# Two transformer blocks on one core: x kept feature-major, the sums into x made with stationary weights

## What is computed

```
def rmsnorm(x, g):
    return x * rsqrt(mean(x * x, axis=-1) + 1e-6) * g

# block 0, layers l = 0, 1                      norms n = 2l, 2l + 1
h = rmsnorm(x, attn_norm[l]); x = x + concat(swa(h), pool(h), mla(h)) @ w_out[l]
h = rmsnorm(x, ffn_norm[l]);  x = x + (silu(h @ w_gate[l]) * (h @ w_up[l])) @ w_down[l]
# block 1, layers l = 0, 1                      norms n = 4 + 2l, 5 + 2l
h = rmsnorm(x, norm_mix[l]);  x = x + mixed(fox(h), nsa(h), gates(h)) @ w_out[l]
h = rmsnorm(x, norm_mlp[l]);  x = x + square(relu(h @ w_up[l])) @ w_down[l]
out = rmsnorm(x, norm_final)
```

## Time and profile before

| | us |
|---|---|
| median of 3 runs (lowest, highest) | 2890.83 (2888.51, 2895.26) |
| profiled execution | 2891.26 |
| its span, first to last instruction | 2889.1 |
| mean granted TensorE clock in it | 0.986 of full |

### The profile page before, as it was taken

The page is one execution under the profiler, slowest core; times in us unless marked ns, Lnnn a source line. Parts: engine busy times, 40 slices in busy tenths (PEclk is TensorE's granted clock), DMA queues, the critical chain, the costliest instruction groups (busy, mean ns, idle before and its releaser), DMA issues.

```text
span 2889.1 us, 34914 instructions
## 1 busy us (share of the span) xinstructions
PE 2754.8 (95%) x13625; PEld 2268.5 (79%) x13625; DVE 1501.4 (52%) x2695; ACT 1158.9 (40%) x2126; POOL 131.3 (5%) x221
## 2 busy tenths in 40 slices
PE   7999999998999999989999999999989899999997
PEld 6777888887778888867777888888767778888886
DVE  6755343357554343565766544343566665543343
ACT  4554222235542222455554343232354644342231
POOL 1000000000000000001022000000011111000000
PEclk9899999999999999999999999999999999999999
DMA  4102332321023323221311223332312211332332
GB/s 123 48 23 77 102 96 95 96 88 55 16 77 101 96 95 96 90 66 45 102 52 44 88 91 99 95 95 95 91 44 81 81 42 54 102 95 95 95 98 77
DMA packets 186358, 231.41 MB, mean 80 GB/s; under 512 B 11874, under 2 KB 140356, under 8 KB 186196
## 3 DMA queue, kind: packets, MB, share of 16 engines
q1 hardware_dynamic: 184500, 225.95, 24.8%
q0 software_dynamic: 976, 1.32, 0.3%
q10 hardware_dynamic: 720, 1.92, 0.2%
HBM read 227.05 MB, written 2.11 MB: 79 GB/s over the span
## 4 chain that ended last, share of the span: by engine, by line
PE 81%; DVE 11%; ACT 4%; issue 3%; DMA 0%; POOL 0%; DVEq 0%; ACTq 0%; SPq 0%
PE bank L643 24%; PE bank L645 23%; PE bank L644 23%; DVE Wl L2126 2%; PE bank L860 1%; PE bank L805 1%; ACT Wh L1416 1%; PE bank L881 1%; DVE STT L2405 1%; PE bank L882 1%; PE bank L742 1%; PE bank L923 1%; PE bank L924 1%; PE bank L790 1%; PE bank L1105 1%
## 5 line engine op out<-in xcount | busy, mean ns | idle before, releaser
L2126 DVE TENSOR_TENSOR Wl<-RAW,Wh 128x1024 fp32r<-128x1024 f32 (+3 forms) x434 | 511.2, 1200 | 369.9 <-ACT Wh L1416 369.0
L1416 ACT ACTIVATE Wh<-RAW 128x1024 fp32r<-128x1024 f32 (+3 forms) x434 | 438.3, 1032 | 368.0 <-PE bank L645 367.4
L643 PE MATMUL bank<-Hh,Wh 128*128 128x512 f32 (+1 forms) x976 | 393.8, 403 | 6.6 <-DVE Wl L2126 5.0
L645 PE MATMUL bank<-Hh,Wl 128*128 128x512 f32 (+1 forms) x976 | 383.5, 393 | 0.0
L644 PE MATMUL bank<-Hl,Wh 128*128 128x512 f32 (+1 forms) x976 | 383.1, 393 | 0.0
L643 PE MATMUL bank<-Wh,A 128*128 128x512 f32 x864 | 337.8, 391 | 0.0
L645 PE MATMUL bank<-Wh,A 128*128 128x512 f32 x864 | 336.8, 390 | 0.0
L644 PE MATMUL bank<-Wl,A 128*128 128x512 f32 x864 | 336.7, 390 | 0.0
L643 PE MATMUL bank<-HA,Wh 128*128 128x512 f32 x704 | 276.5, 393 | 7.5 <-DVE HA L2175 7.5
L645 PE MATMUL bank<-HA,Wl 128*128 128x512 f32 x704 | 275.4, 391 | 0.0
L644 PE MATMUL bank<-HA,Wh 128*128 128x512 f32 x704 | 275.3, 391 | 0.0
(11 more groups left out here) (370 smaller groups left out, 4272.7 us busy)
## 6 DMA issues: line engine op xcount, KB each, us to landing
RAW<-in_w_up_dram SPq DMA_DIRECT2D x108, 512.0 KB, 3.6
RAW<-in_w_down_dram SPq DMA_DIRECT2D x108, 512.0 KB, 3.8
RAW<-in_w_in_dram SPq DMA_DIRECT2D x90, 512.0 KB, 3.5
RAW<-in_w_gate_dram SPq DMA_DIRECT2D x44, 512.0 KB, 3.5
RAW<-in_w_out_dram SPq DMA_DIRECT2D x28, 512.0 KB, 3.8
RAW<-in_cmp_w_dram SPq DMA_DIRECT2D x16, 512.0 KB, 3.9
RAW<-in_w_o_fox_dram SPq DMA_DIRECT2D x8, 512.0 KB, 3.4
RAW<-in_w_o_nsa_dram SPq DMA_DIRECT2D x8, 512.0 KB, 3.4
```

The source lines that it names most:

```text
L643: pe.matmul(o, sh, mh, start=first, stop=False)
L645: return pe.matmul(o, sl, mh, start=False, stop=last)
L1416: sc.activation(M.Wh[:, v % NHL, 0:n], M.RAW[:, v % NRAW, 0:n], ACT.Copy).then_inc(G.w_hi, 1)
L2126: ve.tensor_tensor(M.Wl[:, v % NRAW, 0:n], M.RAW[:, v % NRAW, 0:n], M.Wh[:, v % NHL, 0:n].bitcast(F32), ALU.subtract).then_inc(G.w_lo, 1)
```

## The change

x becomes feature-major, `XT[128, 8, 512]`, from the first turn on.

- `lin_x` (new) makes all sums into x but those of the last feed-forward part. It has the loops of `lin_s` over the same units, but the weights are stationary and the activation moves: four banks of 128 features by 512 tokens. `add_x` adds them to XT (one DVE instruction for each bank) without a factor.
- At a last sum, ACT makes the high part of h(n) from XT right after the addition, and a square of the tile (scaled by 1/1024, no row sum) into `SQX[k]`; DVE makes the low part of the tile before. The turns of norms 1 to 7 are gone; that of n = 0 stays, with an added copy of each bank to XT on ACT.
- GpSimd adds the eight squared tiles of a norm (`add_squares`: seven additions 128x512, each waits for the one before). PE sums over the partitions by token: at the third tick of the product after the sum, four matmuls of one column with `SQS` stationary and ones moving. DVE makes the factors from that bank. The `rb` tile is made for all eight norms, four ticks later.
- The factors are now applied ahead of `down`: block 0 by one more DVE multiplication of the silu tile with rb, block 1 by taking relu on DVE with rb as second factor, with ACT squaring in its place.
- The last feed-forward part keeps `lin_s` and a token-major sum in `XO`. XT is turned back once by eight groups of four transposes (`back_side`) during its first `wide` products, and ACT copies the banks.

The core of the diff, in this order: PE's program (`pe`), ACT's (`sc`), DVE's (`ve`), GpSimd's (`gp`).

```diff
+    def lin_x(name, kt, xh, xl, before=None, often=0):
+        k0, rh, rl = 0, tiles(xh), tiles(xl)
+        while k0 < kt:
+            u, h, lo, ku = next_unit()
...
+            for j in range(NT):
...
+                for k in range(ku):
+                    if before:
+                        before(k0 + k)
+                    i = three(M.bank[bb[j][0]][:, :], h[:, k, j * P:(j + 1) * P], lo[:, k, j * P:(j + 1) * P],
+                              rh[k0 + k], rl[k0 + k], k0 + k == 0, k0 + k == kt - 1)
...
+                tick()
+            k0 += ku
     def normed(n):
         def before(k):
-            if k == 4:
-                drain(turning[n])
-            pe.wait_ge(*K.drained(f"turn{n} {k}"))
+            if n == 0 and k == 4:
+                drain(*turning)
+            pe.wait_ge(G.parted, KD * n + k + 1)
     def factor_side(n):                         
-        yield from idle(5 if n else 8)
-        if n in BY_TOKEN:
+        if n:
+            yield from idle(2)
+            b = fresh(f"ss{n}")
+            pe.wait_ge(G.sqs, 7 * n)
+            for s in range(NT):
+                i = pe.matmul(b[:, s:s + 1], M.SQS[:, s * P:(s + 1) * P], M.ONE[:, 0:1], start=s == 0, stop=s == NT - 1)
+            i.then_inc(*K.fills(f"ss{n}"))
+            yield
+            K.close(f"ss{n}")
+            yield from idle(3)
+        else:
+            yield from idle(8)
+        b = fresh(f"rb{n}")
+        pe.wait_ge(G.rstd, n + 1)
...
+    def back_side():
+        yield from idle(8)
+        for s in range(NT):
+            for half in range(2):
+                b = fresh(f"back {s}{half}")
+                for q in range(4):
+                    i = pe.transpose(b[:, q * P:(q + 1) * P], M.XT[:, 4 * half + q, s * P:(s + 1) * P], ident)
...
     def add_x(half, n=None):
-        def evac(s, name):
+        def evac(j, name):
             if n is not None:
+                k = 4 * half + j
                 sc.wait_ge(*K.drained(name))
-                square_rows(s, half)
+                sc.activation(M.h(n)[0][:, k, :], M.XT[:, k, :], ACT.Copy, scale=M.GT[:, col:col + 1]).then_inc(*hi.up())
+                sc.activation(M.SQX[k], M.XT[:, k, :], ACT.Square, scale=D ** -0.5).then_inc(G.sqx, 1)
     def turn_side(half):
...
+        for k in ks:
+            name = f"turn {k}"
+            sc.wait_ge(G.parted, k + 1)
+            sc.activation(M.XT[:, k, :], M.bank[K.of(name)][:, :], ACT.Copy).then_inc(*K.empties(name))
+    def add_x(half, n=None):
+        def part(k):
+            col = gain_column(n) + k
+            lower(M.h(n)[1][:, k, :], M.XT[:, k, :], M.h(n)[0][:, k, :], M.GT[:, col:col + 1]).then_inc(G.parted, 1)
+        def evac(j, name):
+            k = 4 * half + j
+            ve.wait_ge(*K.full(name))
+            ve.tensor_tensor(M.XT[:, k, :], M.bank[K.of(name)][:, :], M.XT[:, k, :], ALU.add).then_inc(*K.empties(name))
+            if n is not None:
+                if k:
+                    part(k - 1)
+                if k == KD - 1:
+                    part(k)
                     def product(j, name):
+                        ve.wait_ge(*silu.due())
+                        ve.tensor_tensor(m[:, j, :], m[:, j, :], M.rb(n)[:, :], ALU.mult).then_inc(*own.up())
...
+                    def relu(j, name):
...
+                        ve.scalar_tensor_tensor(m, M.bank[K.of(name)][:, :], 0.0, M.rb(n)[:, :], ALU.max, ALU.mult).then_inc(*K.empties(name))
+    def add_squares(n):
+        for k in range(1, KD):
+            gp.wait_ge(G.sqx, KD * (n - 1) + k + 1)
+            if k > 1:
+                gp.wait_ge(*added.now())
+            gp.tensor_tensor(M.SQS, M.SQX[0] if k == 1 else M.SQS, M.SQX[k], ALU.add).then_inc(*added.up())
```

More of the change, by code:

```diff
@@ L588, in norm_of @@
     return 4 * block + 2 * l + place
[L591 to L597, removed]
 def unit_of(plan, u):
@@ L1038, in ffn @@
                     lin_t(f"wide{l} {t}", KD, H[0], H[1], before)
+                if last and t == 0:
+                    back = begin(back_side())
                 before = None
@@ L1044, in down @@
             def down(half):
-                lin_s(f"down{block}{l} {c} {half}", size, A[0], A[1], 512, once(lambda k: pe.wait_ge(G.a_lo, base + k + 1)) if half == 0 else None)
+                name, split = f"down{block}{l} {c} {half}", once(lambda k: pe.wait_ge(G.a_lo, base + k + 1)) if half == 0 else None
+                if last:
+                    lin_s(name, size, A[0], A[1], 512, split)
+                else:
+                    lin_x(name, size, A[0], A[1], split)
+            if last and c == 0:
+                drain(back)
             if x0 == sum(chunks):
@@ L1503, in normed, with back_side @@
+    def factor_side(n):
+        yield from idle(7 if n else 9)
+    def back_side():
+        yield from idle(8)
+        for s in range(NT):
+            for half in range(2):
+                yield
+                name = f"back {s}{half}"
+                sc.wait_ge(*K.full(name))
+                sc.activation(M.XO[:, s, half * 512:half * 512 + 512], M.bank[K.of(name)][:, :], ACT.Copy).then_inc(*K.empties(name))
     def normed(n):
         def before(k):
-            if k == 4:
-                drain(turning[n])
+            if n == 0 and k == 4:
+                drain(*turning)
@@ L1767, in ffn, with squared @@
                 else:
[L1768 removed]
+                    def squared(j, name):
                         m = M.TMP[:, (t + j) % 7, :]
[L1770 to L1774 removed]
+                        sc.wait_ge(*K.drained(name))
+                        sc.activation(m, m, ACT.Square).then_inc(G.a_sq, 1)
+                        sc.wait_ge(*a_sq.due())
                         sc.activation(A[0][:, t + j, :], m, ACT.Copy).then_inc(*hi.up())
[L1776 to L1777 removed]
+                    lin_t(f"wide{l} {x0 + t}", KD, squared, before)
+                if last and t == 0 and c == 0:
+                    back = begin(back_side())
                 before = None
@@ L1781, in down @@
             def down(half):
-                lin_s(f"down{block}{l} {c} {half}", size, add_x(half, n + 1 if x0 == sum(chunks) else None))
+                final = x0 == sum(chunks)
+                lin_s(f"down{block}{l} {c} {half}", size, add_rows(half, final) if last else add_x(half, n + 1 if final else None))
+            if last and c == 0:
+                drain(back)
             if x0 == sum(chunks):
@@ L2706, in down @@
             def down(half):
-                lin_s(f"down{block}{l} {c} {half}", size, add_x(half, n + 1 if x0 == sum(chunks) else None, (n, 1 if gated else 2)))
+                final = x0 == sum(chunks)
+                lin_s(f"down{block}{l} {c} {half}", size, add_rows(half, final) if last else add_x(half, n + 1 if final else None))
+            if last and c == 0:
+                drain(back)
             if x0 == sum(chunks):
```

220 lines of the change are left out of this document (120 added, 100 removed).

## The result

The changed kernel took 2888.17 us, the median of 18 runs (2882.05 to 2892.66), beside 2891.26 us for the kernel before on the same chip (18 runs, 2888.51 to 2895.41). The ratio is 0.9985, interval 0.9978 to 0.9992: 3 us won, where 22 were forecast. It lies 1.2 us above the upper end of the range. The profiled execution took 2891.73 us, with a span of 2889.9 us.

The account below looks back on a forecast made before the run. PE, busy 95% of the span, was taken as the bound. -41 + 3.5 + 3.1 + 3.1 + 4.2 + 2.8 + 2.5 - 0.3 = -22.1 us against 2891.3 gave 2869.2 us, range 2861 to 2887.

Parts of the forecast that it names:

- the wait for the squares: PE's wait for POOL's summed squares at the third tick: 2 us at norms 1 and 3, 0 to 0.2 elsewhere, 4.2 in all.
- The low clock behind waits: Matmuls at the lower clock behind waits at norms 1 and 3: 1.4 us twice, 2.8; bounds 0 and 10 (after every wait).
- The sums over the partitions: Seven groups of four one-column matmuls on PE, priced like a group of turns at 0.44 us: 3.1, bounds 3 to 6.
- the turns of the factors: The rb group on PE, kept five times and new for norms 5 and 7: 7 x 0.44 = 3.1 us.
- The copies at the start: ACT's four copies to XT ahead of the first product: 2.5 us on the path, between 0 and 4.
- the turns' 41 us: Turns of x at seven norms, with the waits on their parts, go from PE: 41 us won.
- the pace of both product forms: Weights stationary or moving, PE's matmuls go at one pace, 0.227 us each, so turning the sums round changes nothing by itself.
- the eight groups of turns back: Eight groups of four turns come back on PE in the last feed-forward part: 8 x 0.44 = 3.5 us.
- More multiplications on DVE: 44 more DVE multiplications (30 us) beside feed-forward products where DVE is about 40% busy; no cost, or 30 if DVE were full.
- A: Rival, chance 0.24: POOL's additions and DVE's two-tensor SBUF work exclude each other; 20 us of waits, 2887 in full, 2884 named.
- lengths that vary widely: Sign in the profile that the forecast is wrong: POOL additions or DVE low parts of widely varying length.
- B: Rival, chance 0.06: POOL's additions in series, 2.5 us each, bound the sum at all seven norms; 2902 us, slower.

Follow-up runs that it names:

- e1: Changed kernel with PE's wait for the summed squares, its one-column products and what hangs on them four ticks (24 matmuls, 5.4 us) later; 2865.66 us.
- e7: e1 with the four one-column products on the sum of squares issued twice at each of the seven norms; 2870.56 us.
- e2: e1, but PE already waits for the summed squares at the third tick, with the products still at the seventh; 2885.75 us.
- e8: e1 with the wait and what follows four ticks later than in the changed kernel at norms 1 and 3 only, two ticks at the others; 2864.96 us.
- e6: e1 with the seven additions of squared tiles of each norm on DVE in place of POOL; 2867.67 us.
- e4: e1 with ACT's first four copies to XT moved behind the first weight units, one ahead of each later high part; 2865.65 us.

## Why the prediction was wrong

- **What failed is the step "the wait for the squares".** It had 4.2 us (2 at norms 1 and 3, 0 to 0.2 elsewhere); the trace has 14.5. The step let POOL's additions run beside DVE's instructions at full speed: with 1.2 us for an addition, "all keep up". The 1.2 was about right, for 1.12 to 1.18 are left of each addition when DVE's share is taken out. That many additions take 1.53, close to the upper bound of 1.54, is chance: DVE's share is in it. What was wrong is the overlap. Each addition waited for DVE first, so a step of the chain took 1.70 in place of 1.2 and no longer kept up with the banks (1.36), and DVE, held up in turn, added the last bank later. An estimate for norm 5 from the rows without this: the last four squares are ready at 1677.93, 1679.29, 1680.65 and 1682.0, the last addition ends at 1683.2 to 1683.4, and PE arrives at 1684.07 and does not wait, where 1.02 was measured. No run has the additions on POOL without contention, so how much of the 14.5 it made stays an estimate: at norms 4 to 7 all of it, by these rows.
- **The low clock behind waits** was 2.8 us in the sum and is 11.4. I left it at the two norms where the kernel before showed it. "Follow every wait (10)" stood beside it as the upper end, and with seven real waits that is near what came.
- **The sums over the partitions**: 3.1 us forecast, 6.8 measured in the changed kernel, 6.3 to 6.6 in e1, and 6.3 for a second set in e7. The turn was the wrong neighbour: a one-column fp32 product leaves two records, and a group of four costs 0.9. None lies within the bounds (3 to 6). (The 5.9 in the forecast of e7 took the turns of the factors at 0.6 each; they are 0.47.)
- **The copies at the start** came 1.5 us onto the first product (2.5 forecast) and 1.4 were still there after 449 matmuls. In these two profiles they seem won back by 231 us (-0.1), but that is luck: the profile of before has a low stretch at 190.8 us, worth 1.6, that the changed kernel's profile lacks and e2's and e8's, with the same start, have.

```profile
189.00:197.00 8.00, 6.29 (x32) 5.38 (x32) 5.87 (x17) 2.79 (x11) 0.00 (x0) 0.79 0.07 22
190.50:198.50 8.00, 6.00 (x39) 4.92 (x38) 6.23 (x19) 3.57 (x13) 0.00 (x0) 1.00 0.12 41
```

(The first line is the kernel before, the second the changed one.)

- **Right**: the turns' 41 us (42.9 by the later count) did go, the pace of both product forms is the old one, the eight groups of turns back lose 3.7 us (3.5), the turns of the factors 3.3 (3.1). More multiplications on DVE cost nothing: the 1212 matmuls from the 671st on take 274.7 us in both kernels.
- **Sum with measured terms**: -42.9 + 14.5 + 1.1 + 11.4 + 6.8 + 3.3 + 3.7 + 1.4 = -0.7, beside a difference of +1.0 between the two traces at the last large matmul. The rest lies in the attention parts, -1.6 at 190 us and +3.3 in block 1, where the low stretches differ from one profile to the next.
- **The rivals.** A named the mechanism that is there, and its sign of being wrong, lengths that vary widely, came: additions of 1.27 to 2.33, low parts of 0.74 to 1.79. Its full form gave 2887, near the 2888 measured, but by luck: 20 us of waits was too high (14.5), and "perhaps 2 of low clock" too low (11.4). The rule of the Trainium skill (SBUF — State Buffer, Who interferes with whom), that a VectorE instruction with two SBUF inputs contends with a GpSimd instruction that reads SBUF and the later one waits, agrees in both directions: with the weight unit at 251.86, which lost 1.06 us of 1.20 beside an addition that had begun before it, and with the addition at 1661.27, which took 1.15 and the 1.18 that DVE had left. B, the additions in series as the bound, had the right place and too high a price (2.5 us each, against 1.70 from one to the next). The Trainium skill (GPSIMD Engine Reference, Performance versus the Vector engine) has a figure for 2048 columns that gave an estimate of 1.12 us for an addition; the trace's 1.12 to 1.18 beyond DVE's share agrees with it. No row shows an addition with nothing beside it.
- **The chances.** 0.47 lay on a wait that needed the overlap to be free, which no row of the trace of before showed, and 0.24 on A. With the measured idle time and low clock in place of 4.2 and 2.8, the prediction's own sum is -22.1 + 10.3 + 8.6 = -3.2 us, beside -3.1 measured; the errors of its other terms about cancel.

## What to carry to other kernels

Where an engine in order has to take the result of a serial chain on a slow engine, place the wait by the chain's worst pace (the length of its instructions with what the other engines do beside them, not alone), and ask what a few ticks more would cost: here four ticks cost nothing and gave 22.5 us. Price a wait of PE of about 1 us or more inside large products, with small products behind it, as the wait plus a low stretch worth 1.7 us or more (it came in 6 of 12 at 1 us, in 5 of 5 at 1.5 to 1.7). When work with SBUF inputs moves to POOL beside DVE instructions with two of them, count for each the rest of the other's instruction as well; then look whether anyone waits for either, since e6 beside e1 shows no cost where nobody does. The best of these kernels, e8 (2864.96) and e1 and e4 beside it (2865.7), are 0.9% faster than the kernel before and 0.8% faster than the change as it was made.

## What the runs showed that was not expected

- A 128x512 fp32 addition of two SBUF tensors on POOL takes what is left of the DVE instruction with two SBUF inputs that it meets and 1.12 to 1.18 us, in 441 of 441 cases; on DVE alone it takes 0.69. A scaling on POOL, with one tensor as input, takes 0.77.
- Four one-column fp32 products (128x128 stationary) take 0.9 us of PE, twice four turns of 128 columns (0.44).
- Two executions of one program, with waits equal to 0.02 us, had low-clock stretches (1.2 GHz) behind three and behind none of norms 4 to 7. That may be part of why the 18 runs of the changed kernel spread over 10.6 us and e1's five over 2.3; it isn't shown, for e7's five, with no such wait, spread over 8.5.
